# A fused decoder step on one core: the first four projection chunks computed side by side, one input tile at a time

## The reference, cut to what matters

```python
h = x                                     # 264 rows of 1024
hn = rmsnorm(h, norm_mix[0])
z = gelu(hn @ w_in)                       # w_in: 1024 x 4096
u, v = split(z, 2, axis=-1)               # v: the last 2048 columns
v = rmsnorm(v, v_norm)
...                                       # gating, FFN, latent attention, FFN, final norm
```

## Time and profile before

| | |
|---|---|
| timed runs, device time | 735.19 us median (734.89 to 735.5) |
| profiled execution, span from first to last instruction | 733.3 us |
| outside the span, to the median of the timed runs | 1.9 us |
| TensorE busy | 724.7 us, 99% of the span |
| ScalarE, VectorE, GpSimd busy | 410.0, 308.4, 534.7 us |
| DMA | 144.68 MB, mean 197 GB/s |

### The profile page before, as it was taken

One profiled execution on the slowest core, in us unless ns is written; L12 is line 12 of the kernel. 1 busy time (PEld: TensorE's weight loads), 2 busy tenths in 40 slices (PEclk: granted clock), 3 DMA queues, 4 the chain that ended last, 5 costly groups with the idle time before them and its releaser, 6 DMA issues.

```text
span 733.3 us, 16703 instructions
## 1 busy us (share of the span) xinstructions
PE 724.7 (99%) x6255; PEld 709.0 (97%) x6255; DVE 308.4 (42%) x781; ACT 410.0 (56%) x747; POOL 534.7 (73%) x252
## 2 busy tenths in 40 slices
PE   9999999999999999999999999999999999999996
PEld 9999999999999999999999888799999999999995
DVE  5446986233333222232588766753233332321002
ACT  7877555455444444555677576564564444444542
POOL 5895778869878888888868122149878888888891
PEclk9999999999999999999999999999999999999999
DMA  7864455656777755666565898326546555555641
GB/s 261 272 201 138 132 166 177 201 173 222 237 235 232 241 179 175 199 202 201 175 255 193 274 373 315 133 66 218 178 148 200 181 188 177 192 175 190 204 153 60
DMA packets 44842, 144.68 MB, mean 197 GB/s; under 512 B 5650, under 2 KB 6674, under 8 KB 44530
## 3 DMA queue, kind: packets, MB, share of 16 engines
q1 hardware_dynamic: 44498, 143.50, 59.0%
q0 software_dynamic: 144, 0.40, 0.1%
q10 hardware_dynamic: 144, 0.02, 0.0%
HBM read 142.42 MB, written 1.48 MB: 196 GB/s over the span
## 4 chain that ended last, share of the span: by engine, by line
PE 95%; DVE 2%; ACT 1%; DMA 1%; issue 0%; SPq 0%; DVEq 0%; ACTq 0%
PE ps L1400 29%; PE ps L1401 29%; PE ps L1402 29%; PE ps L1808 1%; PE ps L1784 1%; PE ps L1728 1%; DMA h<-xT 1%; PE ps L1537 1%; PE ps L1655 0%; PE ps L1446 0%; PE ps L1788 0%; PE ps L1714 0%; ACT whi L485 0%; DVE ps L867 0%; PE ps L1716 0%
## 5 line engine op out<-in xcount | busy, mean ns | idle before, releaser
L419 POOL TENSOR_TENSOR wlo<-raw,whi 128x1024 fp32r<-128x1024 f32 x221 | 527.0, 2406 | 181.5 <-ACT whi L485 181.4
L1400 PE MATMUL ps<-xhi,whi 128*128 128x264 f32 x1000 | 286.2, 286 | 0.0
L1401 PE MATMUL ps<-xlo,whi 128*128 128x264 f32 x1000 | 283.4, 283 | 0.0
L1402 PE MATMUL ps<-xhi,wlo 128*128 128x264 f32 x1000 | 283.2, 283 | 0.0
L485 ACT ACTIVATE whi<-raw 128x1024 fp32r<-128x1024 f32 x221 | 232.7, 1054 | 50.7 <-PE ps L1402 48.6
L1401 PEld LDWEIGHTS ps<-xlo,whi 128*128 128x128 f32 x1000 | 188.5, 188 | 0.1
L1400 PEld LDWEIGHTS ps<-xhi,whi 128*128 128x128 f32 x1000 | 188.3, 188 | 0.3
L1402 PEld LDWEIGHTS ps<-xhi,wlo 128*128 128x128 f32 x1000 | 187.6, 188 | 0.0
L1400 PE MATMUL ps<-ahi,whi 128*128 128x264 f32 x352 | 100.0, 284 | 0.0
L1402 PE MATMUL ps<-ahi,wlo 128*128 128x264 f32 x352 | 99.9, 284 | 0.0
L1401 PE MATMUL ps<-alo,whi 128*128 128x264 f32 x352 | 99.9, 284 | 0.0
(11 more groups left out here) (272 smaller groups left out, 1152.6 us busy)
## 6 DMA issues: line engine op xcount, KB each, us to landing
raw<-w_stream SPq DMA_DIRECT2D x221, 512.0 KB, 3.3
pg<-pages SPq DMA_DIRECT2D x64, 288.0 KB, 4.3
pg<-w_ukT SPq DMA_DIRECT2D x1, 2048.0 KB, 9.4
pg<-w_uv SPq DMA_DIRECT2D x1, 2048.0 KB, 10.2
h<-xT SPq DMA_DIRECT2D x4, 264.0 KB, 4.5
raw<-w_stream SPq DMA_DIRECT2D x4, 256.0 KB, 4.6
y_out<-raw SPq DMA_DIRECT2D x4, 198.0 KB, 2.0
wsraw<-wsT SPq DMA_DIRECT2D x1, 512.0 KB, 5.2
```

Of the source, the lines that this page charges most:

```text
L419: pool.tensor_tensor(wlo[:, c % RING, :], raw[:, c % RING, :], whi[:, c % RING, :].bitcast(F32), ALU.subtract).then_inc(lo_ready, 1)
L1400: pe.matmul(out, whi_, mhi, start=start, stop=False)
L1401: pe.matmul(out, whi_, mlo, start=False, stop=False)
L1402: return pe.matmul(out, wlo_, mhi, start=False, stop=stop)
```

## The change

- The first four slabs are laid out anew in DRAM: half slab k (k = 0 to 7) holds the four blocks of input tile k, one for each of chunks 0 to 3. Slab s consists of half slabs 2s and 2s+1. All of them are loaded in halves, in the order half 0, `h` tiles 0-1, half 1, `h` tiles 2-3, halves 2 and 3, `h` 4-5, halves 4 and 5, `h` 6-7, halves 6 and 7.
- TensorE goes through the eight input tiles once: for tile k four `whi*xhi`, four `whi*xlo` and four `wlo*xhi`, one for each bank 0 to 3. The fillers `held` are gone; `WARM` is 10. The norm's sum stands after the four `whi*xhi` of the last tile.
- ACT splits a half slab after each `xhi` tile and squares the tile before the last; after the squares come slab 4, the root, the gelu table, and only then slab 5.
- DVE takes the low part of the even half slabs, POOL that of the odd ones (128x512 each); DVE adds the squares as they come.
- Slots are freed by `first_used` and `lo_first` for the first round.

```diff
-WARM = 9
+WARM = 10
...
-            sp.dma_start(raw[:, 0, 0:SLAB // 2], w_stream[0][:, 0:SLAB // 2]).then_inc(raw_first, 16)
...
+            def load_half(k):
+                ready = raw_half[k // 2] if k % 2 == 0 else raw_ready[k // 2]
+                sp.dma_start(raw[:, k // 2, half_slab[k % 2]], w_stream[k // 2][:, half_slab[k % 2]]).then_inc(ready, 16)
+
+            load_half(0)
             load_rows(0)
+            load_half(1)
             load_rows(1)
-            sp.dma_start(raw[:, 1, 0:SLAB // 2], w_stream[1][:, 0:SLAB // 2]).then_inc(raw_second, 16)
-            sp.dma_start(raw[:, 0, SLAB // 2:SLAB], w_stream[0][:, SLAB // 2:SLAB]).then_inc(raw_ready[0], 16)
-            load_rows(2)
-            load_rows(3)
-            sp.dma_start(raw[:, 1, SLAB // 2:SLAB], w_stream[1][:, SLAB // 2:SLAB]).then_inc(raw_ready[1], 16)
-            for c in range(2, 2 * RING):
+            for q in range(1, RING):
+                load_half(2 * q)
+                load_half(2 * q + 1)
+                if q + 1 < RING:
+                    load_rows(q + 1)
+            for c in range(RING, 2 * RING):
+                sp.wait_ge(lo_first, c - RING + 1)
                 load(c)
...
-            pool.wait_ge(lo_ready, 2)
-            splits(2, LATER)
+            for s in range(RING):
+                pool.wait_ge(hi_ready, s + 1)
+                pool.tensor_tensor(wlo[:, s, half_slab[1]], raw[:, s, half_slab[1]], whi[:, s, half_slab[1]].bitcast(F32),
+                                   ALU.subtract).then_inc(lo_ready, 1)
+            splits(RING, LATER)
...
-                wait(act, slab_used, c - RING + 1, i, k)
+                if isinstance(i, int) and c + k * i < 2 * RING - 1:
+                    act.wait_ge(first_used, c + k * i - RING + 1)
+                else:
+                    wait(act, slab_used, c - RING + 1, i, k)
...
-            act.wait_ge(gains_in, 16)
...
-            first_split(0, 0, raw_first, hi_first)
-            for m in range(KD // 2):
+            first_split(0)
+            act.wait_ge(gains_in, 16)
+            first_high(0)
+            first_high(1)
+            first_split(1)
+            for m in range(2, KD):
                 first_high(m)
-            first_split(1, 0, raw_second, hi_first)
-            first_split(0, 1, raw_ready[0], hi_ready)
-            for m in range(KD // 2, KD):
-                first_high(m)
-            first_split(1, 1, raw_ready[1], hi_ready)
-            for m in range(KD):
-                act.wait_ge(h_in[m // 2], 16)
-                square(NQ["mix0"], m, h[:, m, :])
-                if m in (1, 5):
-                    split(2 + m // 4)
+                first_split(m)
+                first_square(m - 2)
+            first_square(KD - 2)
+            first_square(KD - 1)
             split(AHEAD + 1)
-            split(AHEAD + 2)
             root("mix0")
             table(ACT.Gelu_apprx_tanh)
+            split(AHEAD + 2)
...
+            gained("mix0", 0, 0)
+            first_slab_low(0)
+            gained("mix0", 1, 1)
+            for m in range(2, KD):
                 gained("mix0", m, m)
-            first_slab_low(0, 1, hi_ready, lo_ready)
-            first_slab_low(1, 1, hi_ready, lo_ready)
-            for m in range(KD):
+                if m % 2 == 0:
+                    first_slab_low(m // 2)
+                add_square(NQ["mix0"], m - 2)
+            for m in range(KD - 2, KD):
                 add_square(NQ["mix0"], m)
             inverse_root("mix0", Ra)
...
+            def row_block(k):
+                s = k // 2
+                ready, low = ((hi_first, lo_first), (hi_ready, lo_ready))[k % 2]
+                at = lambda c: slice((k % 2 * 4 + c) * P, (k % 2 * 4 + c + 1) * P)
+                pe.wait_ge(ready, s + 1)
+                pe.wait_ge(xhi_done, k + 1)
+                for c in range(BANKS):
+                    pe.matmul(ps[:, c, 0:T], whi[:, s, at(c)], xhi[:, k, :], start=k == 0, stop=False)
+                if k == KD - 1:
+                    norm_sum("mix0")
+                pe.wait_ge(xlo_done, k + 1)
+                for c in range(BANKS):
+                    pe.matmul(ps[:, c, 0:T], whi[:, s, at(c)], xlo[:, k, :], start=False, stop=False)
+                pe.wait_ge(low, s + 1)
+                for c in range(BANKS):
+                    last = pe.matmul(ps[:, c, 0:T], wlo[:, s, at(c)], xhi[:, k, :], start=False, stop=k == KD - 1)
...
-            high_first(2)
-            high_first(3, "mix0")
             high_first(4, bank=EARLY_BANK)
...
+    by_rows = value_slabs[:RING].reshape(RING, P, KD, P).transpose(2, 1, 0, 3).reshape(RING, 2, P, SLAB // 2)
```

More of the change, by code:

```diff
@@ L192, in build @@
         pthi, ptlo = (halves(x[:, 4 * NP_:4 * NP_ + 6 * P]) for x in (flat_hi, flat_lo))
+        half_slab = [slice(z * SLAB // 2, (z + 1) * SLAB // 2) for z in range(2)]
         half = [slice(z * T // 2, (z + 1) * T // 2) for z in range(2)]
@@ L239, in build @@
         raw_ready = [sem(f"raw_ready{r}") for r in range(RING)]
-        raw_first, raw_second, hi_first, lo_first = map(sem, ("raw_first", "raw_second", "hi_first", "lo_first"))
+        raw_half = [sem(f"raw_half{r}") for r in range(RING)]
+        hi_first, lo_first, first_used = map(sem, ("hi_first", "lo_first", "first_used"))
         h_in = [sem(f"h_in{q}") for q in range(KD // 2)]
@@ L543, in first_high, with first_split, first_square @@
                 gained("mix0", m)
[L545 to L549, removed]
-            first_split(0, 0, raw_first, hi_first)
-            for m in range(KD // 2):
-                first_high(m)
-            first_split(1, 0, raw_second, hi_first)
-            first_split(0, 1, raw_ready[0], hi_ready)
-            for m in range(KD // 2, KD):
-                first_high(m)
-            first_split(1, 1, raw_ready[1], hi_ready)
-            for m in range(KD):
-                act.wait_ge(h_in[m // 2], 16)
-                square(NQ["mix0"], m, h[:, m, :])
-                if m in (1, 5):
-                    split(2 + m // 4)
+            def first_split(k):
+                ready, done = ((raw_half, hi_first), (raw_ready, hi_ready))[k % 2]
+                act.wait_ge(ready[k // 2], 16)
+                act.activation(whi[:, k // 2, half_slab[k % 2]], raw[:, k // 2, half_slab[k % 2]], ACT.Copy).then_inc(done, 1)
+            def first_square(m):
+                square(NQ["mix0"], m, h[:, m, :])
+            first_split(0)
[4 more added lines that the diff above has]
+            for m in range(2, KD):
+                first_high(m)
+                first_split(m)
+                first_square(m - 2)
+            first_square(KD - 2)
+            first_square(KD - 1)
             split(AHEAD + 1)
-            split(AHEAD + 2)
             root("mix0")
             table(ACT.Gelu_apprx_tanh)
+            split(AHEAD + 2)
             def vt_hi(u_, i):
@@ L917, in _, with first_slab_low @@
             dve.wait_ge(gains_in, 16)
[L919 to L925, removed]
-                gained("mix0", m, m)
[L927 to L930, removed]
-            first_slab_low(0, 1, hi_ready, lo_ready)
-            first_slab_low(1, 1, hi_ready, lo_ready)
-            for m in range(KD):
+            def first_slab_low(s):
+                dve.wait_ge(hi_first, s + 1)
+                lo_of(wlo[:, s, half_slab[0]], raw[:, s, half_slab[0]], whi[:, s, half_slab[0]]).then_inc(lo_first, 1)
+            gained("mix0", 0, 0)
+            first_slab_low(0)
+            gained("mix0", 1, 1)
+            for m in range(2, KD):
+                gained("mix0", m, m)
+                if m % 2 == 0:
+                    first_slab_low(m // 2)
+                add_square(NQ["mix0"], m - 2)
+            for m in range(KD - 2, KD):
                 add_square(NQ["mix0"], m)
@@ L1456, in _, with high_products @@
             pe.wait_ge(const_done, 9)
[L1457 to L1462, removed]
+            def row_block(k):
[14 more added lines that the diff above has]
+                    last = pe.matmul(ps[:, c, 0:T], wlo[:, s, at(c)], xhi[:, k, :], start=False, stop=k == KD - 1)
+                    if k == KD - 1:
+                        last.then_inc(slab_used, 1)
+                if k % 2 and k < KD - 1:
+                    last.then_inc(first_used, 1)
+            for k in range(KD):
+                row_block(k)
+            def high_products(c, half, bank=None):
                 out = ps[:, c % BANKS if bank is None else bank, 0:T]
@@ L1466, in high_products @@
                     w = slice(b * P, b * P + P)
-                    if rows:
-                        rows(b)
                     pe.matmul(out, whi[:, c % RING, w], xhi[:, b, :], start=b == 0, stop=False)
@@ L1479, in low_products, with high_first @@
                     last.then_inc(slab_used, 1)
[L1481 to L1500, removed]
+            def high_first(c, bank=None):
                 pe.wait_ge(hi_ready, c + 1)
                 high_products(c, 0, bank=bank)
-                if between:
```

(6 more changed lines are left out.)

## The result

| | median of 16 runs | lowest to highest | profiled span |
|---|---|---|---|
| before | 735.27 us | 734.88 to 735.5 | 733.3 us |
| changed | 736.59 us | 736.13 to 737.23 | 735.0 us |

The changed kernel takes 1.0018 times as long, 95% interval 1.0011 to 1.0024: 1.3 us slower, within the 0.2% that the prediction called no change, but clear of zero and outside the range of 733.6 to 736.0. I had forecast 0.3 us less.

The account below looks back on a forecast made before the run. TensorE, busy 99%, was taken to bound the kernel, with a start chain nearly as late. Its -1.53 us was to shrink to -0.32 as the turns came at 25.42 instead of 25.74: 734.9 us, range 733.6 to 736.0.

Parts of the forecast that it names:

- What bounds the start: First 26 us: TensorE never short of work, but a chain over squares, root, gelu and scaling nearly as late (0.2 us wait).
- TensorE's part: Start on TensorE: fillers go, first block at 5.38 us, full rate from 6.1; -1.53 us in all if TensorE waits for nothing.
- Does it wait among the blocks?: Side-by-side blocks: each engine's work under 1.46 us a block, so no stall; norm's sum starts at about 16.45 us.
- my row: ScalarE's predicted path from taking half slab 2 at 7.52 us to the norm's sum at 16.45: 8.93 us.
- The late landings: Rival: pieces land 1.03 us apart, last half slab at 14.7 us, turns 0.9 later; +0.57, 735.8 us; chance 0.09.
- The table: Rival: after the gelu table load ACT stands still another 1.3 us, turns at 26.7; 736.2 us; chance 0.02.
- TensorE's clock: Rival: clock falls to 1.2 GHz in the new 1.4 us wait before the turns, costing 2.45 us; 737.3 us; chance 0.04.
- TensorE keeping the whole gain: Rival: the whole -1.53 us on TensorE survives to the end, needing the first gelu by 18.74 us; 733.66 us; chance 0.15.

Follow-up runs that it names:

- e15: Changed kernel with TensorE's chunk 6 put ahead of the wait before turn_v(1) and turn_v(2), turn_v(3) behind chunk 7; 735.56 us, ratio 1.0002.
- e11: Changed kernel with the last xlo behind the last three additions of squares and ScalarE's slab 6 split moved behind chunk 0's transposed copy; 735.43 us, ratio 0.9999.
- e2: Changed kernel with GpSimd's four half-slab subtractions replaced by a memset of the same 128x512, writing but reading nothing; one run, 735.54 us.
- e3: Changed kernel with GpSimd's four half-slab subtractions replaced by a copy of the same 128x512, one input, so low parts are wrong; one run, 735.37 us.
- e17: Kernel before with one unused GpSimd subtraction of 128x512 added, started when the fifth xhi is ready; 736.60 us, ratio 1.0019.

## Why the prediction was wrong, point by point

- **What bounds the start** was read rightly: the gain on TensorE ends at the row from the sum over the root and ScalarE to the turns. From the sum to the turns I had 8.97 us; the changed kernel has 27.33 - 18.28 = 9.05. e15 shows the wait there to be worth 1.0 us of device time, and e11 that the row is ScalarE's work.
- **TensorE's part** began as forecast (first block at 5.43, I had 5.38) and then came late: block 1 starts at 7.76 (7.17), because the starts stayed at the 1.2 GHz distance, 0.22 us apart, until 7.1 us and not until 6.1; block 7 starts at 16.60 (15.94). In the other nine profiles of the new order that distance ended between 4.0 and 7.1 us; where it ended early, short waits for `xhi`, `xlo` or `whi` came instead, and in none does block 7 start before 16.39. This error of 0.45 us or more was hidden behind the wait for VectorE. Without that wait the sum could have started at 17.09 in the changed kernel's profile, not at 16.45.
- **The step that failed** is the one that began "Does it wait among the blocks?" and took VectorE's 0.41 us per `xlo` and GpSimd's 1.2 us per half slab each for itself, "all are under 1.46 a block". The 0.41 was from rows beside which GpSimd did next to nothing: it was idle from 5.9 to 12.5 us in the kernel before. In the changed kernel three of GpSimd's four subtractions start in exactly that time. The measured rows show such a subtraction and an `xlo` going nearly one after the other. Taken so, four subtractions of 1.3 us and eight `xlo` and four low parts of VectorE are, as an estimate from the rows, 5.2 + 3.3 + 2.4 = 10.9 us of work in the 11 us from 5.4 to 16.5, while ScalarE's squares wait for additions that stand behind. It cost 10.30 - 8.93 = **1.37 us** at the sum against my row. The other 0.46 us of the 1.83 is the landing of half slab 2 at 7.98, and behind the sum 0.08 more. Against the rows without a hold-up (8.76 in e2, 8.77 in e3) it is 1.54: my row was 0.17 too long without it. One price in it that was too high is the addition, 0.55 in the prediction; from 13.93 to 14.27 the next instruction follows it after 0.34.
- **What the runs show without the hold-up.** The single runs e2 and e3 took 735.54 and 735.37 us, 1.1 and 1.2 less than the changed kernel, and still 0.5 and 0.3 more than the kernel before in their group. Their sums start at 17.28 and 17.05 and not at 16.45. So the hold-up is the larger part of the miss, and the rest (the late landings, and TensorE's blocks behind them) is more than the 0.32 us that I had forecast as a gain.
- **A price was to be had** in the trace of before. I took the earlier trace rows for the price of an `xlo` and left out the others. VectorE's timeline, layer 0's FFN, has

```profile
120.12 2.73 DVE L909 SCALAR_TENSOR_TENSOR xlo<-h,gn,xhi 128x264 fp32r<-128x264 f32 x1
```

and GpSimd's timeline beside it

```profile
117.81 7.31 POOL L419 TENSOR_TENSOR wlo<-raw,whi 128x1024 fp32r<-128x1024 f32 x3 [2.28 <-ACT whi L485]
```

  The same instruction on the same shape, over five times as long beside GpSimd, in a place where TensorE has no wait.
- **Rivals.** The late landings came in part (0.46 of the 0.9 us priced), and alone would have left the kernel within the range (-0.32 + 0.46 = +0.14 us). The table cost its row's 1.28 us and no more. TensorE's clock did not fall in the waits of 1.03 and 1.31 us: from 18.95 and from 27.95 us on products start 0.12 us apart again, and the single longer distances ahead of these (0.31 and 0.21) stand behind the norm's sum and a turn in the kernel before as well. TensorE keeping the whole gain was never near.
- **The forecast** of -0.32 us became +1.32. With 1.37 added for the hold-up and 0.46 for the landing it would have been +1.5. That this comes close is not a full account, since TensorE's own lateness lies under the same wait.

## What to carry to other kernels

Before giving work to an engine that a stretch of the trace shows idle, look at what the others read in that stretch: a duration taken beside an idle neighbour is not the duration beside a busy one, so ask for the smallest and the largest time of each instruction and where the largest stands. Work that looks balanced engine by engine can be too much where two engines' instructions hold each other up, and the order within a queue then decides what it costs: moving one `xlo` behind three additions won back 1.0 us. And where a faster start runs into a long row of small dependent steps, put independent products ahead of the wait (e15) before shortening what comes in front of it.

## What the runs showed of the hardware that I had not expected

- A VectorE instruction with two SBUF inputs is held up for the rest of a GpSimd instruction that reads SBUF with one or two inputs (0.83 us beside a copy of 0.61, up to 1.60 beside a subtraction of 1.30), and not by one that only writes (0.48 beside a memset of 0.53). Additions with one input in PSUM kept 0.43 us, as the one at 15.27 us beside the subtraction of 14.90 to 16.50.
- GpSimd can pay as well: its subtraction took 1.60 us instead of 1.3 where it came second to VectorE's half slab at 14.67. Where the two start 0.02 us apart, either can pay: in the changed kernel's profile the `xlo` of 12.40 took 1.60 and the subtraction of 12.42 took 1.30; in e15 it was the other way round, as VectorE's and GpSimd's timelines show:

```profile
12.47 0.48 DVE L923 SCALAR_TENSOR_TENSOR xlo<-h,gn,xhi 128x264 fp32r<-128x264 f32 x1
```

```profile
12.49 1.61 POOL L465 TENSOR_TENSOR wlo<-raw,whi 128x512 fp32r<-128x512 f32 x1 [1.18 <-ACT whi L562]
```

- One such meeting, of an instruction whose output is not used, cost a kernel that is 99% busy on TensorE 1.5 us by the medians and 1.0 by the profile (e17).
- A 256 KB transfer that stands fifth in the queue was taken up at 7.5 to 8.7 us over the profiles of this case.
